# Decay levels of a linear-attention decoder kernel: the projection beside them in two pieces of 24 matmuls a level in place of three

## The reference

```python
proj = rms_norm(h, norm_pre_mix) @ w_in      # columns: hq hf hi hg | aq ak av | gq gk gv lr gr
o_h, s = gated_linear_recurrence(hq, 1 - f, hi, log(f), s_hgrn)       # 4 heads
o_a = dilated_window_attention(rotary(aq), rotary(ak) + cache, ...)   # 6 heads
o_g, s = gated_linear_recurrence(gq, gk, gv, log_a, s_gla)            # 6 heads
h = h + rms_norm(concat(o_h, o_a, o_g) @ w_out)
h = h + rms_norm(square(relu(rms_norm(h) @ w_up)) @ w_down)
h = h + sigmoid(h @ w_ple_gate) * (p @ w_ple)
# inside gated_linear_recurrence, for each chunk of 64 tokens, b = cumsum(log f):
A = einsum('bthk,bshk,btshk->bths', q, k, exp(b_t - b_s), causal)
o = (q * exp(b)) @ S + A @ v
```

## Time and profile before

| | |
|---|---|
| median of 3 runs | 1723.86 us (1722.9 to 1727.79) |
| the profiled execution, its own time | 1726.31 us |
| its span, first to last instruction | 1724.5 us |
| PE, DVE, ACT, POOL busy in the span | 1665.3, 1106.3, 699.4, 91.0 us |
| mean granted clock of TensorE | 0.982 of full speed |
| decay levels, first to last couple, layer 0 | 172.7 to 250.0 us |
| decay levels, layer 1 | 1030.9 to 1106.1 us |

### The profile page before, as it was taken

One profiled execution on the slowest core, in us unless ns is written; L12 is line 12 of the kernel. 1 busy time (PEld: TensorE's weight loads), 2 busy tenths in 40 slices (PEclk: granted clock), 3 DMA queues, 4 the chain that ended last, 5 costly groups with the idle time before them and its releaser, 6 DMA issues.

```text
span 1724.5 us, 36328 instructions
## 1 busy us (share of the span) xinstructions
PE 1665.3 (97%) x15770; PEld 1541.5 (89%) x15770; DVE 1106.3 (64%) x1789; ACT 699.4 (41%) x1040; POOL 91.0 (5%) x102
## 2 busy tenths in 40 slices
PE   9999898899999999998999999988999999999988
PEld 8888885599999999998998888755999999999988
DVE  6624885436877777776746258764368777777674
ACT  5431435545533333333543223355454333333342
POOL 0002200000000000001000121000000000000010
PEclk9999999999999999999999989999999999999999
DMA  9411549933936635542372124597349356554411
GB/s 335 154 66 57 182 163 349 351 129 116 354 100 242 244 135 208 202 154 77 127 275 80 62 72 154 209 364 290 129 157 340 117 207 235 200 197 165 154 62 68
DMA packets 61662, 314.02 MB, mean 182 GB/s; under 512 B 7232, under 2 KB 8896, under 8 KB 59328
## 3 DMA queue, kind: packets, MB, share of 16 engines
q1 hardware_dynamic: 53792, 206.51, 33.2%
q0 software_dynamic: 7424, 100.47, 16.3%
q10 hardware_dynamic: 288, 4.72, 0.6%
HBM read 296.34 MB, written 115.80 MB: 239 GB/s over the span
## 4 chain that ended last, share of the span: by engine, by line
PE 86%; DVE 7%; ACT 3%; DMA 2%; issue 1%; POOL 1%; SPq 0%; DVEq 0%; ACTq 0%
PE pair L2109 7%; PE pair L2111 7%; PE pair L2110 7%; PE pair L2097 6%; PE pair L2099 6%; PE pair L2098 6%; PE pair L937 2%; PE pair L939 2%; PE pair L941 2%; PE pair L1989 2%; PE pair L854 2%; PE pair L1991 2%; PE pair L1990 2%; PE pair L1226 2%; PE pair L856 2%; PE pair L855 2%
## 5 line engine op out<-in xcount | busy, mean ns | idle before, releaser
L2109 PE MATMUL pair<-u_hi_part,w_hi_part 128*128 128x288 f32 x1024 | 302.5, 295 | 1.5 <-DVE y L2523 1.5
L2111 PE MATMUL pair<-u_hi_part,w_lo_part 128*128 128x288 f32 x1024 | 302.0, 295 | 0.0
L2110 PE MATMUL pair<-u_lo_part,w_hi_part 128*128 128x288 f32 x1024 | 301.5, 294 | 0.0
L2425 DVE TENSOR_TENSOR w_lo_part<-raw,w_hi_part 128x1024 fp32r<-128x1024 f32 (+1 forms) x148 | 167.2, 1130 | 81.6 <-ACT w_hi_part L2213 78.1
L2109 PEld LDWEIGHTS pair<-u_hi_part,w_hi_part 128*128 128x128 f32 x1024 | 192.1, 188 | 2.7 <-DVE y L2523 2.4
L2110 PEld LDWEIGHTS pair<-u_lo_part,w_hi_part 128*128 128x128 f32 x1024 | 192.1, 188 | 0.1
L2111 PEld LDWEIGHTS pair<-u_hi_part,w_lo_part 128*128 128x128 f32 x1024 | 192.1, 188 | 0.0
L2213 ACT ACTIVATE w_hi_part<-raw 128x1024 fp32r<-128x1024 f32 (+1 forms) x154 | 148.8, 981 | 86.4 <-PE pair L2099 80.0
L2099 PE MATMUL pair<-x_hi_part,w_lo_part 128*128 128x288 f32 x416 | 122.6, 295 | 0.0
L2098 PE MATMUL pair<-x_lo_part,w_hi_part 128*128 128x288 f32 x416 | 122.4, 294 | 0.0
L2097 PE MATMUL pair<-x_hi_part,w_hi_part 128*128 128x288 f32 x416 | 122.3, 294 | 0.0
(11 more groups left out here) (333 smaller groups left out, 4364.6 us busy)
## 6 DMA issues: line engine op xcount, KB each, us to landing
raw<-w_units SPq DMA_DIRECT2D x210, 512.0 KB, 3.8
ck_out<-ck POOLq DMA_DIRECT2D x16, 3060.0 KB, 15.7
arena<-cv SPq DMA_DIRECT2D x24, 640.0 KB, 8.7
arena<-ck SPq DMA_DIRECT2D x18, 640.0 KB, 9.6
more<-ck SPq DMA_DIRECT2D x18, 640.0 KB, 11.9
tail<-cv SPq DMA_DIRECT2D x18, 640.0 KB, 7.9
h<-ck SPq DMA_DIRECT2D x12, 640.0 KB, 10.1
y_out<-x ACTq DMA_DIRECT2D x2, 2304.0 KB, 9.8
```

What stands on the lines that cost most here:

```text
L2109: nc.tensor.matmul(out, wh[:, cols], UH[:, u, t], start=first and k == 0, stop=False)
L2110: nc.tensor.matmul(out, wh[:, cols], UL[:, u, t], start=False, stop=False)
L2111: mm = nc.tensor.matmul(out, wl[:, cols], UH[:, u, t], start=False, stop=last and k == KD - 1)
L2425: return tt_(dst, src, hi.bitcast(F32), ALU.subtract).then_inc(*up(done, 1))
```

## The change

A unit of the projection goes in two pieces. Before: 18 matmuls between couples 0 and 1, 15 between couples 1 and 2, and 15 after couple 2. After: 24 between couples 0 and 1, none between couples 1 and 2, and 24 after couple 2.

```diff
                     for first in range(0, len(GROUPS), 2):
                         if l >= 4 and first >= 2:
                             partners(2 * (l - 4) + first // 4)
-                        if first >= 2 and l < len(LEVELS) - 1:
-                            project(5 + l, *((0, 18) if first == 2 else (18, 33)))
+                        if first == 2 and l < len(LEVELS) - 1:
+                            project(5 + l, 0, 24)
                         if gi >= 2:
                             pe.wait_ge(*at(lv_ev, gi))
...
                     if l < len(LEVELS) - 1:
-                        project(5 + l, 33)
+                        project(5 + l, 24)
```

## The result

The changed kernel takes 1736.45 us (median of 17 runs, 1732.51 to 1743.44), the one before 1727.79 us (17 runs, 1722.9 to 1736.15). The ratio is 1.0049, with a 95% interval of 1.0035 to 1.0064: **0.5% slower**. By the ratio that is 8.5 us, and so differences in us are given from here on. The change was timed a second time with the last experiments, with a ratio of 1.0067 (1.0046 to 1.0088), 11.6 us. The forecast was 10.7 us more, and 1734.6 us in all, counted from a median of three runs that turned out 3.9 us under the median of 17.

What follows compares the result with a forecast made beforehand. TensorE, busy for 97% of the span, was taken to bound the kernel. Waits of 6.2 us plus clock falls of 4.5 us made 10.7 us on the median of 1723.86, so 1734.6 us, range 1729.0 to 1740.

Steps and rivals of the forecast that it cites:

- Level 0, nothing: Level 1's couple 0 comes about 1.2 us later at no cost, as DVE waits for POOL's gate products anyway.
- the cover: PE's 2.49 us idle time in level 1, said to hide the later couple 0; without it, 1.2 us more.
- Levels 1 to 3, 1.20 + 1.20 + 0.70 us: Couple 2 waits for DVE's picks and moved matmuls follow it: 3.1 us a layer, 6.2 us in both.
- The share of four picks: Level 3: couple 2 waits for three of DVE's four copies of couple 1, taken as 0.9 us, bounds 0.7 and 1.01.
- Levels 4 and 5, nothing: The rotation between couples 1 and 2 hides DVE's pick with 0.3 us to spare: 0, bounds 0 and +0.4 each.
- The clock, three further falls of 1.5 us, 4.5 us: TensorE's clock falls after gaps of 2 us or more: level 1 in layer 1, level 2 in both layers.
- Waits only: Rival: the clock adds one fall at most; +6.2 to +7.7 us, 1730 to 1731.6 us; chance 0.22.
- Clock in every level: Rival: five more falls than now in levels 1 to 3, 7.5 us; +13.7 us, 1737.6 us; chance 0.15.
- Absorbed: Rival: cache loads after the levels set the mixer's end and make up the delay; about 1724 to 1728 us; chance 0.10.
- Faster: Rival: the shift moves low-clock stretches after the levels onto idle time; about 1718 us; chance 0.03.

Runs made afterwards that it cites:

- the run with 20 filling matmuls: Changed kernel plus 12, 20, 12 and 4 unread matmuls between couples 1 and 2 of levels 0 to 3; 1739.47 us, ratio 1.0067.
- the control of the last experiment: Kernel before, with the second rotation product of levels 4 to 6 moved behind couple 2; one execution, 1729.14 us.
- PE kept at work: Changed kernel plus 10, 7, 8 and 3 unread matmuls between couples 1 and 2 of levels 0 to 3; 1733.93 us, ratio 1.0038.
- the rotation moved: Changed kernel, with the second rotation product of levels 4 to 6 moved behind couple 2; one execution, 1756.6 us.
- the two edits together: Changed kernel with couple 2 in the two banks of the free projection pair; 1720.39 us, ratio 0.9960, repeated at 1724.36 us, ratio 0.9979.

## Why the prediction was right, step by step

**Level 0, nothing.** Right to within half a microsecond. The clock's fall in level 0 had not been counted. It brings level 1's couple 0 up to 4.2 us late in place of 1.2 and uses the cover up: couple 1 of level 1, which was not to move, starts 19.86 and 18.59 us after level 0's couple 0 (before 17.66) and no longer waits. Couple 2 moves little: 23.11 and 22.86 us (before 22.84 and 22.86), 23.34 and 23.26 in the second profile. So its wait, forecast at 3.9 us, is 1.89 and 2.91.

**Levels 1 to 3, 1.20 + 1.20 + 0.70 us.** Level 2 was to be 12.02 us and is 11.99 to 12.02 wherever the clock held; level 3 was to be 10.94 and is 10.97. The step from couple 2 to the next couple 0 was to be 4.10 us and is (223.00 to 227.10). The share of four picks after which couple 2 starts, taken at 0.9 us in level 3, is 0.92. Level 1 has no clean reading, as in the changed kernel it never ran without a fall. The nearest is layer 1 of the run with 20 filling matmuls, at full clock: 12.44 + 15.60 us for levels 0 and 1, of which 0.81 is the halt, so 27.2. The forecast's waits put on level 1 without an exposed fall give 25.77 + 1.20 = 27.0.

**Levels 4 and 5, nothing.** Right (11.60 and 11.62 us); couple 2 comes 2.23 us after couple 1, forecast 2.2.

**The clock, three further falls of 1.5 us, 4.5 us.** The sum is near, its parts less so. The count came out: four falls lie on the path in the profile after (level 1 and level 2 of each layer), one in that before. That is in part luck: gaps of 0.84 and 0.86 us had falls too, and so had level 0's, which was not counted. From the four passes of the changed kernel, levels 0 and 1 take 29.05 us in the mean. Four passes with the old order there (the two of before, 27.25 and 25.77, and the control of the last experiment, 27.04 and 27.24) take 26.83. That is 2.2 us a layer, of which 1.2 is wait by the forecast's reckoning. Levels 2 and 3 add 24.5 - 21.05 = 3.4 us, of which 1.9 is wait. Both layers give 2 x (2.2 + 3.4) = 11.3 us: 6.2 of waits, 5.1 of clock. The price of one fall was off where it meets a longer piece: from couple 2 to the next couple 0, level 1 of layer 1 took 1066.44 - 1059.67 = 6.8 us in place of 4.1, not 5.6. The 1.5 us were read from a piece of 15; 24 matmuls at 0.238 in place of 0.133 us make 2.5. And a gap of 0.86 us, which I had counted out, sometimes has the fall in place of the 1.89 us one: in eight passes with the new order in levels 2 and 3 there was one fall each, six times in level 2 and twice in level 3.

**The rivals.** Waits only: ruled out by levels 2 and 3, 24.5 us against 22.98 with PE kept at work. Clock in every level: not that often; in each pair of levels 2 and 3, with a wait in both, there was one fall. But the rule of the Trainium skill (TensorE: Matmul & The Clock Gate, section "A second HAM failure mode: psum-queue depth-cycling"), that short idle times between groups make the clock go down and up, is nearer to these runs than I gave it credit for: with the rotation moved it fell in levels 4 and 5 too. Absorbed: no; the key loads moved with the stage (SP issues the second group at 250.42 us, before at 244.27, as late as level 6's couple 0), and from there to layer 1's levels it is as long as before, within 0.3 us. Faster: no.

What stays open is how the 13.5 us between the two profiles, the 11.3 us of the windows and the ratios' 8.5 and 11.6 us fit exactly. Runs of one kernel differ by 10 us and more, and a profile is one of them.

## What to carry to other kernels

When two groups of matmuls share a bank, whatever stands between them is the cover for the engine that empties it. Before it is moved, compare the time from the group's start to the end of the emptying with what is left in between; work that is moved behind a wait that another engine ends is added in full. Where the groups can have banks of their own, take the wait away first: only then did fewer, longer pieces pay here, and the two edits together gave 0.2 to 0.4% where each alone gave nothing or a loss.

## What the runs showed of the hardware

A wait of under 1 us with only small matmuls on both sides of it can be followed by a fall of the clock: in the run with the rotation moved it fell in four of four levels with 0.84 us of waiting, at 1.4 us each. It need not: behind the 0.86 us of level 3 it fell in two of eight passes.

Matmuls put into a wait did not always hold the clock. With 8 and 3 of them in levels 2 and 3, 0.66 and 0.27 us of waiting were left, and it held; 7 of them in level 1 left 2.70 us, and it fell. After a fall, work put into the next wait can become the path itself: behind a wait of 2.48 us matmuls took 0.24 us each in place of 0.13.

PE stood still for up to 2.31 us within a group of matmuls with no wait that the profile shows, and the clock fell in that halt (granted 0.50 from 205 us). A total in which this happens says little of the edit.
